# A new order of the attention pipeline's steps in a four-layer fp32 transformer kernel

## What is computed

```python
def _dsa(q, k, v, qi, ki, wi):              # 4 "a" heads, one shared key and value head
    score = sum_h wi * relu(qi @ ki) ; causal
    _, sel = lax.top_k(score, 128)          # per query
    softmax over the selected keys only, then @ v
def _stick_breaking(q, k, v):               # 4 "b" heads
    z = q @ k * scale ; log_keep = log_sigmoid(-z) on strict keys
    a = exp(log_sigmoid(z) + reverse_cumsum(log_keep) - log_keep)
    return a @ v
def _swa_sinks(q, k, v, sinks):             # 8 "c" heads, window of 128, sinks
    ...
o = _rms(concat([oa, ob, oc]), g_out) ; x = x + g1 * (o @ w_o)
x = x + g2 * swiglu(norm(x))
```

## Time and profile before

| | before |
|---|---|
| median of 3 runs | 3133.03 us (3124.57 to 3137.35) |
| profiled execution: its time | 3130.37 us |
| its span in the profile | 3128.6 us |
| PE busy | 2908.3 us (93%) |
| DVE busy | 1787.2 us (57%) |
| POOL busy | 931.1 us (30%) |
| ACT busy | 756.2 us (24%) |
| granted TensorE clock, mean | 0.951 |

### The profile page before, as it was taken

One profiled execution on the slowest core, in us unless ns is written; L12 is line 12 of the kernel. 1 busy time (PEld: TensorE's weight loads), 2 busy tenths in 40 slices (PEclk: granted clock), 3 DMA queues, 4 the chain that ended last, 5 costly groups with the idle time before them and its releaser, 6 DMA issues.

```text
span 3128.6 us, 33693 instructions
## 1 busy us (share of the span) xinstructions
PE 2908.3 (93%) x12126; PEld 2133.1 (68%) x12126; DVE 1787.2 (57%) x3803; ACT 756.2 (24%) x1781; POOL 931.1 (30%) x794
## 2 busy tenths in 40 slices
PE   8888999999997899999989988999999998899997
PEld 4354688888544578888854456888884454688886
DVE  2673469388367447938854545877824634551433
ACT  2354310000235431000022353201112335320111
POOL 0301224443330124444412202344440400344442
PEclk9989999999998799999989988999999998899998
DMA  6115034244221013434421101254421210122221
GB/s 256 64 61 215 28 138 166 101 148 170 91 80 61 1 55 121 175 108 156 154 76 56 61 27 68 108 183 186 156 100 57 59 50 23 40 94 96 81 81 54
DMA packets 45412, 313.28 MB, mean 100 GB/s; under 512 B 5424, under 2 KB 5552, under 8 KB 31040
## 3 DMA queue, kind: packets, MB, share of 16 engines
q1 hardware_dynamic: 42912, 306.88, 27.0%
q10 hardware_dynamic: 2304, 4.20, 0.6%
q0 software_dynamic: 32, 0.07, 0.0%
HBM read 298.53 MB, written 2.10 MB: 96 GB/s over the span
## 4 chain that ended last, share of the span: by engine, by line
PE 70%; DVE 18%; ACT 6%; issue 3%; DMA 1%; POOL 1%; DVEq 0%; SPq 0%; ACTq 0%; POOLq 0%
PE bank L1114 39%; PE bank L1094 9%; PE bank L1440 7%; PE bank L1168 3%; DVE nw L2067 3%; PE bank L1264 2%; DVE sel L2304 2%; DVE m L2303 1%; PE bank L1307 1%; DVE SPT L2368 1%; ACT SPT L1756 1%; PE bank L1294 1%; PE bank L1229 1%; PE bank L1567 1%; DMA sel<-in_mod_pieces 1%
## 5 line engine op out<-in xcount | busy, mean ns | idle before, releaser
L1000 POOL TENSOR_TENSOR SPT<-ring 128x512 f32<-128x512 f32 (+2 forms) x140 | 175.2, 1252 | 956.3 <-DMA ring<-in_slabs 493.0
L1114 PE MATMUL bank<-U,ring 128*128 128x256 f32 x1728 | 412.2, 384 | 10.8 <-DVE U L2101 10.5
L1114 PEld LDWEIGHTS bank<-U,ring 128*128 128x128 f32 x1728 | 332.8, 193 | 58.4 <-DVE U L2101 12.5
L2067 DVE SCALAR_TENSOR_TENSOR nw<-sel,c,nw 128x256 f32<-128x256 f32 x504 | 321.7, 638 | 31.2 <-DMA sel<-in_mod_pieces 13.5
L1114 PE MATMUL bank<-U,SPT 128*128 128x256 f32 x1296 | 312.5, 381 | 3.0 <-POOL SPT L1005 3.0
L1114 PEld LDWEIGHTS bank<-U,SPT 128*128 128x128 f32 x1296 | 247.4, 191 | 37.7 <-POOL SPT L1005 4.4
L1114 PE MATMUL bank<-hT,SPT 128*128 128x256 f32 x1088 | 257.1, 379 | 0.0
L1440 PE MATMUL bank<-hT,ring 128*128 128x512 f32 x544 | 249.7, 607 | 7.1 <-ACT hT L1873 7.1
L2127 DVE TENSOR_TENSOR rb<-bank,nw 128x256 f32<-128x256 f32 x108 | 45.5, 422 | 355.9 <-PE bank L1114 259.1
L1114 PE MATMUL bank<-hT,ring 128*128 128x256 f32 x1088 | 246.1, 379 | 0.0
L1114 PEld LDWEIGHTS bank<-hT,ring 128*128 128x128 f32 x1088 | 207.0, 190 | 28.0 <-DMA ring<-in_slabs 0.3
(11 more groups left out here) (344 smaller groups left out, 4501.9 us busy)
## 6 DMA issues: line engine op xcount, KB each, us to landing
ring<-in_slabs SPq DMA_DIRECT2D x86, 2048.0 KB, 8.0
sel<-in_mod_pieces SPq DMA_DIRECT2D x144, 512.0 KB, 4.5
ring<-in_slabs SPq DMA_DIRECT2D x8, 1536.0 KB, 7.0
ring<-in_slabs SPq DMA_DIRECT2D x8, 1280.0 KB, 8.3
tab<-U SPq DMA_DIRECT2D x40, 128.0 KB, 2.0
U<-in_slabs SPq DMA_DIRECT2D x2, 2048.0 KB, 22.5
tmp<-nw ACTq DMA_DIRECT2D x16, 256.0 KB, 2.9
ring<-in_slabs SPq DMA_DIRECT2D x2, 1808.0 KB, 11.7
```

Of the source, the lines that this page charges most:

```text
L1000: pool.tensor_tensor(e1, a21, a22, ALU.add).then_inc(*pool_order.up())
L1114: mm = pe.matmul(into[j][:, c:c + HALF], lhs[:, k, :], rhs[:, k, :], start=(begin and k == 0), stop=(end and k == kp - 1))
L2067: ins = dve.scalar_tensor_tensor(a, w[:, k, :], c[:, j:j + 1], a, ALU.mult, ALU.add)
```

## The change

The change alters the lists, not the arithmetic.

1. In `group_slots` a slot becomes, in order: `ot` of j-4, `pv` of j-2, `ln` of j-3, `sc` of j; then `rd` of j-2, `on` of j-3, `tp` of j-1. `ln` is the ACT part of what was `on`, and `rd` is the DVE part of what was `pv`. So ACT does copy and squares of `pv` and the roots ahead of the exponents of `sc`, and DVE does sums and scaling behind the mask of `sc`. The pipeline is one slot longer. DVE waits before `sc` of g for its own scaling of g-4.
2. `group_slots2` gets the same, with `cb` of j-1 behind `sc` of j and ahead of `tp` of j-1.
3. The index key tile comes first: `TILES1` begins 2, 0, 1. `projv` runs in the order 1, 2, 3, 0, the first of them after tile 1, the others between the `idx` steps, and each `idx` step of DVE waits for its own `projv` alone. The rounds start behind `idx 1`, three behind each `idx`.
4. The two woven stretches of block 1 become one: tiles in its first half, fourteen groups over 0.2 to 0.95, rounds over 0 to 0.5, stick-breaking heads over 0.5 to 0.96, mod products over 0.45 to 0.74, `wo 0` in the last quarter. Six group steps `sc` (0 to 5) stand ahead of the first mod product, where eight whole groups stood before.
5. The DMAs of `rope`, the slabs' columns and the waits on the last `projv` follow the new order.

```diff
-TILES1 = (0, 1, 2, 10, 12, 13, 14, 15, 4, 5, 6, 7, 8, 9)
+TILES1 = (2, 0, 1, 10, 12, 13, 14, 15, 4, 5, 6, 7, 8, 9)
+V_ORDER = (1, 2, 3, 0)
-TURNED_BEHIND = {("v", 0): ROPED[:2], ("kq", 0): ROPED[2:3], ("qa", 0): ROPED[3:6], ("qb", 0): ROPED[6:]}
+TURNED_BEHIND = {("v", 0): ROPED[:3], ("kq", 0): ROPED[3:4], ("qa", 0): ROPED[4:7], ("qb", 0): ROPED[7:]}
 def group_slots(groups):
-    for j in range(len(groups) + 3):
-        early, late = [], []
-        if 0 <= j - 3 < len(groups):
-            early.append(("on", groups[j - 3]))
-        if j < len(groups):
-            early.append(("sc", groups[j]))
-        if 0 <= j - 2 < len(groups):
-            late.append(("pv", groups[j - 2]))
-        if 0 <= j - 1 < len(groups):
-            late.append(("tp", groups[j - 1]))
-        if 0 <= j - 3 < len(groups):
-            late.append(("ot", groups[j - 3]))
+    for j in range(len(groups) + 4):
+        back = {d: groups[j - d] for d in range(5) if 0 <= j - d < len(groups)}
+        early = [(kind, back[d]) for kind, d in (("ot", 4), ("pv", 2), ("ln", 3), ("sc", 0)) if d in back]
+        late = [(kind, back[d]) for kind, d in (("rd", 2), ("on", 3), ("tp", 1)) if d in back]
...
-    for m in range(6):
+    for m in range(4):
...
+        if m == 2:
+            o += [("projv", V_ORDER[0])]
+    o += [("rope", TILES1[2])]
+    for i in range(1, QT):
+        o += [("idx", i, hp) for hp in range(2)] + [("projv", V_ORDER[i])]
+        o += [st for chunk_ in rounds[3 * i - 3:3 * i] for st in chunk_]
+        if i == 1:
+            o += [("pss", KC)]
+    rounds = rounds[9:] + [[("seldone", i)] for i in range(1, QT)]
...
-    o += woven((-0.03, 0.92, dense), (0.37, 1.01, group_slots(range(NC1))),
-               (0, 1.15, rounds + [[("seldone", i)] for i in range(1, QT)]))
...
-    o += woven((0, 0.96, stick_slots()), (0.08, 0.95, group_slots(range(NC1, len(GROUPS1)))),
-               (0, 0.55, mods), (0.55 if l == 0 else 0.1, 1, [[("wo", 0, n)] for n in range(KT)]))
+    o += woven((-0.01, 0.48, dense), (0.2, 0.95, group_slots(range(len(GROUPS1)))), (0, 0.2, rounds[:18]),
+               (0.2, 0.5, rounds[18:]), (0.5, 0.96, stick_slots()), (0.45, 0.74, mods),
+               (0.74 if l == 0 else 0.68, 1.02, [[("wo", 0, n)] for n in range(KT)]))
...
 def group_slots2(groups):
...
+        early = [(kind, back[d]) for kind, d in (("ot", 4), ("pv", 2), ("ln", 3), ("sc", 0))
+                 if d in back and (kind != "ot" or back[d] in TURNS2)]
+        late = [(kind, back[d]) for kind, d in (("cb", 1), ("rd", 2), ("on", 3), ("tp", 1))
+                if d in back and (kind != "cb" or GROUPS2[back[d]][0] == "d")]
...
-                        if i == 1 and hp == 0:
-                            for j in range(QT):
-                                dve.wait_ge(*bk1.taken(l, ("projv", j)))
+                        if hp == 0:
+                            dve.wait_ge(*bk1.taken(l, ("projv", i)))
...
+                        if g >= 4:
+                            dve.wait_ge(*s1["un"].after(l, g - 3))
```

More of the change, by code:

```diff
@@ L506, in group_slots2 @@
     out = []
-    for j in range(len(groups) + 3):
-        early, late = [], []
-        if 0 <= j - 3 < len(groups):
-            early.append(("on", groups[j - 3]))
-        if 0 <= j - 1 < len(groups) and GROUPS2[groups[j - 1]][0] == "d":
-            early.append(("cb", groups[j - 1]))
-        if j < len(groups):
-            early.append(("sc", groups[j]))
-        if 0 <= j - 2 < len(groups):
-            late.append(("pv", groups[j - 2]))
-        if 0 <= j - 1 < len(groups):
-            late.append(("tp", groups[j - 1]))
-        if 0 <= j - 3 < len(groups) and groups[j - 3] in TURNS2:
-            late.append(("ot", groups[j - 3]))
+    for j in range(len(groups) + 4):
+        back = {d: groups[j - d] for d in range(5) if 0 <= j - d < len(groups)}
+        early = [(kind, back[d]) for kind, d in (("ot", 4), ("pv", 2), ("ln", 3), ("sc", 0))
+                 if d in back and (kind != "ot" or back[d] in TURNS2)]
+        late = [(kind, back[d]) for kind, d in (("cb", 1), ("rd", 2), ("on", 3), ("tp", 1))
+                if d in back and (kind != "cb" or GROUPS2[back[d]][0] == "d")]
         out.append([early, late])
@@ L1957, in _ @@
                                            ACT.Square).then_inc(*s2["uq"].up())
-                    elif kind == "on" and GROUPS2[st[1]][0] == "d":
+                    elif kind == "ln" and GROUPS2[st[1]][0] == "d":
                         g = st[1]
```

51 lines of the change are left out of this document (23 added, 28 removed).

## The result

The changed kernel takes **3205.1 us** (median of 4 runs, 3203.32 to 3209.59) against 3133.92 before: a ratio of 1.023, 95% interval 1.021 to 1.026. It is 71 us slower where I had forecast 40 faster. The profiled execution has a span of 3201.5 us (3128.6 before); PE is busy 2949.3 us, 41 more, and stands idle 252 us, 32 more; the mean granted clock is 0.939 (0.951). DVE's busy time is 1793.0 (1787.2).

What follows compares the result with a forecast made beforehand. In block 1's mixings DVE was taken to bound each layer's first part, PE the second. From 3130.37 us, block 1 takes off 58 and block 2 adds 20: 3092, left as 3093 us, range 3070 to 3112.

Steps and rivals of the forecast that it cites:

- Part 1: Block 1, layer start: DVE's first index sum comes +39.2 us after PE's first tile, not +57.3, so 18 us earlier.
- the cover of 4 us: Block 1, layer start: index keys are roped at +34 us, 4 us ahead of the index scores at +37.7.
- Part 2: Block 1, each layer's first part: less DVE work ends it at about +155 us in layer 0, gaining 43 us (layer 1: 39).
- Part 3: Block 1, each layer's second part: PE takes over 14 us, 142 us in layer 0; net gain 29 us a layer.
- rival (b): Block 1, DVE's part: early start eaten by waits, or POOL holds DVE; gain only 30 us, 3120 us total; chance 0.12.
- The lower end of the gain: Block 1, layer 0's first part: with 24 us of DVE idle, the gain is 36 us instead of 43.
- the 20 that I had named as a sign of being wrong: Block 1, layer 0: the prediction is wrong if the second part grows by over 20 us.
- The squares: Block 1, groups: DVE's 20.3 us a layer of waits for ACT's squares fall under 5.
- Part 4: Block 2, "d" groups: PE's turns wait some 2.5 us for `cb` behind the mask; 10 us lost a layer, 20 in all.
- Rival (c): Block 2, "d" stretch: stalls keep the clock at its lower level, +66 us a layer, 3204 us total; chance 0.07.
- (a): Block 2 gains instead, the removed tie outweighing the wait: -10 us a layer, 3052 us total; chance 0.17.
- (d): Whole kernel: the reorder does nothing, since PE is the limit anyway, 3130 us; chance 0.04.

Runs made afterwards that it cites:

- the new start alone: Key tile first, value products between index steps, early rounds, against the kernel before; its two stretches and old slots kept: 3119.93 us, ratio 0.9969.

## Why the prediction was wrong, point by point

**Part 1 was right.** First index sum at +36.4 (+39.2 forecast), PE's index scores without a wait for the keys, so the cover of 4 us held.

**Part 2 failed in its reading of the bound.** I saw DVE busy 54.32 of 64.20 and 61.49 of 77.83 us and called the part DVE's, then summed DVE's work alone to +155. PE was busy 54.11 and 65.18 us in the same windows, 119.3 us against DVE's 115.8, and all of the 55.83 us from the first tile to 93.80: 175.1 in all. With the 14 us of Part 3 moved out, 161 us of PE work stay in a part that I let end at 155. The sum of my own rows forbade it. After the change PE has 156.6 us of work there and 10.2 of idle, +166.8. The run with the new start alone shows it purest: 18 us sooner on DVE bring 4.8 us.

In the terms of my sum, DVE's 104 us of work were right: 103.5 from its first index sum to the hand-over. The term that failed is its idle time, 13 us with 24 as upper end. It is 27.0 us, 12.9 of them in four waits for ACT's roots of tiles; ACT in turn waits there for PE's sums of these tiles, 15.2 us in seven waits. So the first half of rival (b) came true: part of what DVE wins at its start is handed back as waits for PE. The lower end of the gain was also summed wrongly: 24 us of idle give a hand-over at +166 and a gain of 32, not 36.

**Part 3, right in kind, mis-sized.** 14 us of moved work were to make 142. Measured 159.8: the busy time there is 141.4, which is 114.3, 14, some 4.5 that I had not counted as moved (175.1 - 156.6 = 18.5 left the first part), and 8.6 left over, for which the clock of 0.88 in place of 0.95 is more than enough; the rest is 4.5 us more idle. (Of the 4.5, 3.3 are the stick-breaking score that stood ahead of my cut.) The part grew by 31.6 us, past the 20 that I had named as a sign of being wrong. In layer 1 I had looked at the gaps as room for the moved work, but not at what lies in them: the one stretch sets wo 0 late there, as the list of steps shows without any run, and late wo 0 by itself costs 14 us in the layout with two stretches.

**The squares.** 20.3 us of waits under 5: right, they are gone. That it saves time was wrong. The squares come early only because `pv` stands ahead of `sc`, and I had priced that at "a few us, within the 5". Where slots stand close, `ot` and `pv` ahead of `sc` cost 20 us of the 23 that the new slots add (the two runs of the new start that differ in this); in the one stretch, where other steps lie between, the slots cost nothing. My claim that the steps between cover it was right for the layout that I was predicting and for no other.

**Part 4, right in mechanism, a third of the size: the step that cost most.** The wait for `cb` is there in nine slots with 25.9 us (20 to 25 forecast). The stretch grew by 33.4 and not 10. My sum, from `sc 6` to the end, was 5 x 5.9 + 3 x 8.3 + 5.9 + 2 x 6.3 + 17 = 90 us; its terms measure, in order, 39.5, 33.0, 6.2, 16.3 and 20.2, 115.2 in all. The most mis-sized term is the slot without wo 0: I wrote 5.2 to 5.9 us. The five such slots from 1823.02 to the first product at 1867.44 take 44.42 us with a piece of the sixth; start to start they are 8.5, 6.0, 7.5, 9.2 and 8.3, mean 7.9. The one of the timeline above is 4.3 us of PE work (0.66, 0.45 for `ot`, 1.09 for `pv`, 2.08) and 3.5 of waits: I had not added the wait to the work. Next come the three slots with a product on the wrong side, 11.1, 10.3 and 11.7 us for my 8.3, whose products take 5.3 to 5.8 us where the earlier trace rows has 3.60. The second omission is `pv` at the head of the slot, 28 us in two layers, which my Part 4 did not name. The third is the clock: 11.3 us of the 33.4 are products that take longer at a lower one. These three overlap and don't add up. Rival (c) had this mechanism and put it at +66 a layer; it came at half of that, with 0.72 for the stretch, on the border that it named itself. Its total of 3204 us is the measured one by luck: it has +132 for block 2 and -58 for block 1, where the runs show +65 and +11.

**Rivals.** (a) fell: without `cb`'s and `pv`'s waits the rest of the new order gives 0.9996. Of (b), the half with POOL holding DVE fell: DVE's busy time rose by 6 us in all. (d) had right that PE was nearly the limit already. The total of +71 came from block 2 (+65 alone) and block 1 (+11 alone), in whose trace layer 1 loses 14; my chance of 0.08 for slower was far too small, as it rested on one mechanism in one block.

**Left open.** The one stretch also loses 11 us in layer 0 with old slots (794.1 against 783.3 from layer to layer), where wo 0 is not late. The last section shows that this much can come and go there by the clock alone, and no run here tells the two apart. Whether late wo 0 is what layer 1 loses in the one stretch is argued from the other layout, not shown. Of the 23 us of the run with wo 0 late in layer 1 alone, the 9 beyond that layer's 14 are open in the same way. A version with new start and `pv` behind the scores in layer 1 only (in the run that has it in both layers, layer 1 takes 972.3 us to the first "d" scores, where the start alone has 984.5) was not tried.

## What to carry to other kernels

Before a stage is put down to one engine, sum the other engine's work in the same window: a stage can't end before the busiest one's remaining work, whatever starts earlier. In a pipeline in which all engines walk one list and the slots stand close, put the step that feeds the other engines (the scores) ahead of every step that waits for what the last slot's scores led to; a step moved ahead of it is paid by all engines in turn. Long products that depend on nothing recent are worth more than their own time when they stand between short dependent ones: spread them over the stretch. Set late in both layers they cost 26 us here, set earlier 8 to 10.

## What the runs showed of the hardware

I had not expected how far the clock moves over identical code. From the first `bz` to the last `bot` of layer 0, the list of steps is the same in these three runs: the kernel before, the new slots in block 2 alone (its block 1 is that of before), and the new start with wo 0 late in layer 1 only.

```profile
232.54:359.13 126.59, 113.53 (x606) 67.17 (x605) 52.64 (x150) 53.98 (x126) 13.70 (x32) 0.94 0.36 133
```

```profile
230.23:366.30 136.07, 124.47 (x606) 74.08 (x605) 52.78 (x150) 54.35 (x126) 13.69 (x32) 0.85 0.33 124
```

```profile
228.31:369.55 141.24, 130.46 (x606) 76.87 (x605) 52.75 (x150) 54.68 (x126) 13.71 (x32) 0.81 0.32 120
```

PE is idle 13.1, 11.6 and 10.8 us: no more, rather less. Its 606 products take 113.5, 124.5 and 130.5 us as the granted clock is 0.94, 0.85 and 0.81, so the stretch differs by up to 15 us with nothing changed in it. (The third trace is of the slowest of that version's ten executions, 3152.66 us at a median of 3142.72.) Layer 1's counterpart stays at 0.82 and 115.7 to 115.9 us in four of the five traces with before's block 1, and is 111.5 at 0.85 in the fifth. Why the clock differs no run here shows. A single profile of a stage with many short waits is thus good to some 10 us here. The readings above that are smaller than that and rest on windows, such as the 4.8 us of the new start and the 9 of the new slots, are only as good; which version is faster is told by the medians of whole runs.
